# Taking 47 unread identity products off TensorE's queue in a two-block network on one core

## The reference, cut to what matters

```python
# first block, DEPTH = 2
for i in range(DEPTH):
    xn = rms_norm(h, norm_mix[i])
    h = h + (moba_attention(xn, ...) if i % 2 == 0 else rwkv7_time_mix(xn, ...))
    h = h + conv_ffn(rms_norm(h, norm_ffn[i]), ...)
x = rms_norm(h, norm_final)

# second block, DEPTH = 2
for l in range(DEPTH):
    h = rmsnorm(x, ln1_g[l]) * (1.0 + sc1) + sh1
    z = h @ w_in[l]
    xr, yr, q, k, v = jnp.split(z, splits, axis=-1)
    lru = rg_lru(causal_conv(xr, ...), ...) * jax.nn.gelu(yr)
    att = diff_attention(q, k, v, ...)
    x = x + g1 * (jnp.concatenate([lru, att], axis=-1) @ w_out[l])
    h = rmsnorm(x, ln2_g[l]) * (1.0 + sc2) + sh2
    f = swiglu(h, ...) if l % 2 == 0 else moe(h, moe_router[0], ...)   # 8 experts, top 2
    x = x + g2 * f
return rmsnorm(x, final_g)

def rms_norm(x, g):
    y = x * lax.rsqrt(jnp.mean(x * x, axis=-1, keepdims=True) + EPS)
    return y * g
```

## Time and profile before

| | before |
|---|---|
| median of 3 runs | 2081.14 us (2078.46 to 2083.44) |
| profiled execution, own time | 2088.03 us |
| its span | 2086.2 us |
| mean granted TensorE clock over the span | 0.985 |
| PE busy | 2030.1 us (97%), 12388 products in the trace |
| DVE, ACT busy | 1717.7 us (82%), 1257.7 us (60%) |
| HBM read | 531.47 MB, 255 GB/s over the span |

### The profile page before, as it was taken

One profiled execution on the slowest core, in us unless ns is written; L12 is line 12 of the kernel. 1 busy time (PEld: TensorE's weight loads), 2 busy tenths in 40 slices (PEclk: granted clock), 3 DMA queues, 4 the chain that ended last, 5 costly groups with the idle time before them and its releaser, 6 DMA issues. The chain is left out here.

```text
span 2086.2 us, 31412 instructions
## 1 busy us (share of the span) xinstructions
PE 2030.1 (97%) x12388; PEld 1759.5 (84%) x12389; DVE 1717.7 (82%) x1983; ACT 1257.7 (60%) x1282; POOL 45.5 (2%) x84
## 2 busy tenths in 40 slices
PE   9999999999899999999999999999999999999998
PEld 8889997988799988799998878888888788888876
DVE  6868887886788877778788788988898889989997
ACT  5564447643444356643445777777777777777775
POOL 0000000000000000000000000000000000000000
PEclk9999999998899999999999999999999999999999
DMA  7358862201477644378874259998999899999995
GB/s 279 122 209 278 308 228 76 103 22 44 179 282 263 246 136 169 124 293 302 305 258 147 101 210 374 360 368 324 377 354 370 321 367 361 355 350 366 362 343 212
DMA packets 79466, 534.53 MB, mean 256 GB/s; under 512 B 11840, under 2 KB 13120, under 8 KB 15584
## 3 DMA queue, kind: packets, MB, share of 16 engines
q1 hardware_dynamic: 71744, 481.04, 62.3%
q0 software_dynamic: 7440, 51.49, 6.7%
q10 hardware_dynamic: 144, 0.02, 0.0%
HBM read 531.47 MB, written 1.05 MB: 255 GB/s over the span
## 5 line engine op out<-in xcount | busy, mean ns | idle before, releaser
L2454 DVE TENSOR_TENSOR weights_lo<-ring,weights_hi 128x2048 fp32r<-128x2048 f32 x193 | 436.7, 2280 | 64.0 <-ACT weights_hi L2448 63.7
L826 PE MATMUL bank<-acts_hi,weights_hi 128*128 128x256 f32 x1584 | 454.2, 287 | 6.3 <-DVE acts_lo L425 3.8
L403 DVE TENSOR_TENSOR weights_lo<-ring,weights_hi 128x2048 fp32r<-128x2048 f32 x161 | 368.0, 2290 | 110.0 <-ACT weights_hi L393 108.8
L393 ACT CAST weights_hi<-ring 128x2048 fp32r<-128x2048 f32 x161 | 307.0, 1908 | 249.5 <-PE bank L826 224.6
L826 PE MATMUL bank<-acts_lo,weights_hi 128*128 128x256 f32 x1584 | 448.1, 283 | 0.0
L826 PE MATMUL bank<-acts_hi,weights_lo 128*128 128x256 f32 x1584 | 448.0, 283 | 0.0
L2448 ACT CAST weights_hi<-ring 128x2048 fp32r<-128x2048 f32 x192 | 367.3, 1917 | 80.8 <-PE bank L2969 50.1
L826 PEld LDWEIGHTS bank<-acts_hi,weights_hi 128*128 128x128 f32 x1584 | 303.6, 192 | 14.6 <-issue 11.5
L2969 PE MATMUL bank<-weights_hi,xg_hi 128*128 128x512 f32 x768 | 305.3, 398 | 7.1 <-issue 3.3
L826 PEld LDWEIGHTS bank<-acts_lo,weights_hi 128*128 128x128 f32 x1584 | 303.8, 192 | 2.6 <-issue 1.4
L826 PEld LDWEIGHTS bank<-acts_hi,weights_lo 128*128 128x128 f32 x1584 | 303.8, 192 | 0.0
(11 more groups left out here) (500 smaller groups left out, 2869.8 us busy)
## 6 DMA issues: line engine op xcount, KB each, us to landing
ring<-in_experts SPq DMA_DIRECT2D x192, 1024.0 KB, 6.6
ring<-in_dense SPq DMA_DIRECT2D x162, 1024.0 KB, 4.9
ring_more<-in_experts SPq DMA_DIRECT2D x96, 1024.0 KB, 6.7
ada<-in_ada POOLq DMA_DIRECT2D x48, 1024.0 KB, 5.2
silu_c<-in_c SPq DMA_DIRECT2D x3, 512.0 KB, 6.4
resid<-in_x SPq DMA_DIRECT2D x2, 512.0 KB, 4.3
out<-resid SPq DMA_DIRECT2D x4, 256.0 KB, 2.1
small<-in_consts SPq DMA_DIRECT2D x1, 649.5 KB, 10.3
```

What stands on the lines that cost most here:

```text
L393: nc.scalar.copy(split[0][:, n % SPLITS, :], ring[:, n % RING, :]).then_inc(hi_ready, 1)
L403: nc.vector.tensor_tensor(split[1][:, n % SPLITS, :], ring[:, n % RING, :], split[0][:, n % SPLITS, :].bitcast(F32), ALU.subtract).then_in ...
L826: ins = nc.tensor.matmul(bank[:, f * T:(f + 1) * T], split[w][:, m % SPLITS, k * 256 + f * P:k * 256 + (f + 1) * P], acts[x][:, k, :], sta ...
L2454: ins = nc.vector.tensor_tensor(split[1][:, at, lo:hi], place(j)[0][:, lo:hi], split[0][:, at, lo:hi].bitcast(F32), ALU.subtract)
```

## The change

All calls of `keep_busy`, the function itself and the arguments that carried its counts are taken out. No other line is changed.

```diff
@@ -431,15 +431,6 @@
-        def keep_busy(bank, count, wide=True):
-
-            for _ in range(count):
-                if wide:
-                    nc.tensor.matmul(pb[bank][:], ident, const("cos", 0, 2 * T), start=True, stop=True)
-                else:
-                    nc.tensor.matmul(pb[bank][:, 0:P], ident, ident, start=True, stop=True)
@@ -563,9 +554,8 @@
-            def pe(self, pe, before=0, behind=0):
+            def pe(self, pe):
                 done = self.normed
-                keep_busy(3, before)
                 for t in range(TT):
...
-                keep_busy(4, behind)
@@ -972,7 +961,6 @@
                     pe.wait_ge(early_in, 16)
-                    keep_busy(7, 10, wide=False)
                     norm.pe(pe)
@@ -1397,7 +1385,7 @@
                         pe.wait_ge(ada_read, tb + len(turns))
-                        norm.pe(pe, *((2, 3), (6, 2), (3, 2))[name])
+                        norm.pe(pe)
@@ -2119,7 +2107,6 @@
                     ins.then_inc(bonus_done, 1)
 
-                    keep_busy(7, 11)
                     pe.wait_ge(x_ready, 1)
                     pe.wait_ge(bonus_out, 2)
@@ -2617,7 +2604,6 @@
                         project(pe, n1 + 1, 1, 4, acts)
-                        keep_busy(3, 2)
                         if routes:
@@ -2630,7 +2616,7 @@
                             project(pe, n1 + c, c, 4, acts)
-                        norm.pe(pe, *((2, 2), (4, 1))[l])
+                        norm.pe(pe)
@@ -3021,7 +3007,6 @@
                 if kind in ("last", "extra"):
-                    keep_busy(4, 3, wide=False)
                     scatter_weighed(pe, n + 1)
@@ -3258,7 +3243,6 @@
                     sel = w3[2]
-                    keep_busy(7, 3)
                     pe.wait_ge(r_top, 1)
@@ -3266,9 +3250,7 @@
                     pe.wait_ge(normed, normed_made[0])
-                    keep_busy(7, 1)
                     gather(pe, 0, 2)
-                    keep_busy(7, 1)
                     all_passes(pe, pe_pass)
```

## The result

| | before | after |
|---|---|---|
| median of 20 runs each | 2082.13 us | 2088.80 us |
| ratio after/before, 95% interval | | 1.0032 [1.0023, 1.0041] |
| profiled execution, its span | 2088.03, 2086.2 us | 2084.07, 2082.3 us |
| mean granted clock in it | 0.985 | 0.978 |

The forecast was 2086.6 us with 5.5 us more than before; measured are 6.7 more. One of the 20 runs of after took 3315.45 us at a granted clock of 0.554 and is left out of the ratio; without it the median is 2088.32 us, 6.2 above that of before.

The account below looks back on a forecast made before the run. TensorE was taken to bound the kernel, 36 of the 42% of span the wait chain covers. Terms -3.4 + (1.7 + 1.9 + 2.3 + 0.6) + 0.8 + 0 + 1.6 + 0 = +5.5 on 2081.1 gave 2086.6 us; whole range 2078 to 2093.

Parts of the forecast that it names:

- mixers, both: Second block's mixers, at 862 and 1190: products stand on the path; transposes start 1.7 us earlier, twice: -3.4 us.
- norm 324: Norm at 324: cover lost, but a later wait for VectorE's mix swallows most: +0.6 us, from 0 to 1.7.
- norm 765: Norm at 765: 9.8 us with two norms in it, clock falls: +2.3 us, from 0 to 3.4.
- norm 880: Norm at 880: fall expected, dense products pay 1.5 us plus 0.2 for transposes: +1.7 us, between 0 and 3.3.
- norm 1095: Norm at 1095: stretch to the next product like that at 880, at 7.2 us: +1.9 us.
- the four norms: Norms at 324, 765, 880, 1095: products in spare time, removal wins nothing and loses clock cover: 6.5 us.
- start: Kernel's start: transposes and first products run at half speed, a later transfer wait swallows over 1 us: +0.8, 0 to 2.7.
- recurrent stage: Recurrent stage: about 1.1 us won at once, 32-wide products start at 1.2 GHz: 0, from -1.1 to +1.5 us.
- router: Router: without its three products the gather behind begins at 1.2 GHz: +1.6 us, from 0 to 3.4.
- First rival, the clock holds: At the norms transposes break the pauses, so their 6.5 us fall away: -1.0, or 2080 us; chance 20%.
- Second rival, no cover lost: Identity products cost path and cover nothing; mixers win 6.4 us, recurrent stage 1.1: 2073.6 us; chance 8%.
- Third rival, transposes do not hold the clock: Each norm is one bare pause of 7 to 10 us: +13.1, or 2094 us; chance 9%.

Follow-up runs that it names:

- mixers_moved: Kernel before with the mixers' four identity products moved, one behind each of the four norms' transposes: 2078.13 us, ratio 0.9981 [0.9972, 0.9989].
- lean: Kernel before less the unread products of the mixers, the first norm (324), the start and the end: 2080.27 us, ratio 0.9990 [0.9980, 0.9999].
- norms_out: Kernel before less only the identity products at the four norms: 2087.48 us, ratio 1.0027 [1.0016, 1.0038].
- rest_out: Kernel before less only the products at the start, in the recurrent stage, around the router and at the end: 2081.74 us, ratio 1.0004 [0.9995, 1.0013].
- mixers_out: Kernel before less only the identity products in the two mixers' output projections: 2085.76 us, ratio 1.0023 [1.0013, 1.0033].
- norms_kept: Kernel before less all unread products except those of the four norms: 2079.10 us, ratio 0.9989 [0.9980, 0.9998].
- norms_turned: Kernel before with each wide identity product at the four norms replaced by eight unread transposes: 2080.20 us, ratio 0.9994 [0.9983, 1.0005].
- recurrent_seven: Kernel before with 7 of the 11 products in the recurrent stage kept, all else unchanged: 2093.31 us, ratio 1.0052 [1.0033, 1.0070].

## Why the prediction was right

Its account was: the mixers' products cost path, the norms' cost nothing and hold the clock, and the second outweighs the first. By step, in us; the profile's column is one execution of after against one of before, each place measured against what precedes it; the last column is a kernel's difference in median, or, where it says so, a mean over the twelve profiles:

| place | predicted | profile of after | kernels |
|---|---|---|---|
| mixers, both | -3.4 | -1.7 and -1.7 | -3.5 (mixers_moved) |
| norm 324 | +0.6 | 0 | 0 (profiles of lean, norms_out) |
| norm 765 | +2.3 | +2.9 | |
| norm 880 | +1.7 | +2.7 | |
| norm 1095 | +1.9 | +1.0 | |
| the four norms | +6.5 | +6.6 | +7.2 (norms_out) |
| start | +0.8 | 0 | +0.7 (profiles) |
| recurrent stage | 0 | -0.3 | |
| router | +1.6 | +1.5 | +1.0 (profiles) |
| these three and the end | +2.4 | +1.2 | +1.4 (rest_out) |
| sum | +5.5 | +4.4 | +6.7 (the change) |

*Mixers.* Right to 0.1 us in the trace: the first product behind the transposes went from 867.34 to 863.62 and the transposes from 864.08 to 860.37, 3.7 us, of which 2.0 were there before the mixer. That the falls at 868 and 1196 may come or not was right too: after has the first alone; mixers_out has neither.

*Norms.* The mechanism is shown: falls where the products are gone (after, norms_out), none where they stay or transposes replace them (norms_kept, norms_turned). Three sizes were off. At 324 nothing is lost, where I had 0.6: the later pause swallows a fall whole. At 880 I had one fall, and there were two, the first over the transposes: the last product in front of the norm stood 3.7 earlier than before, the first feed-forward product only 2.27 earlier (884.74 against 887.01), which is 1.4 in the norm, and the second fall took 1.3 more. At 1095 the fall lay over the transposes only and ended in the pause behind them: the last product in front stood 1.03 earlier (1093.59 against 1094.62), the first behind 0.19 later, 1.2 lost, of which 0.25 is back ten microseconds on, and no dense product was at 1.2 GHz. I had charged each norm for dense products at half speed; the transposes at half speed were in my account with 0.2. They take 1.3 to 1.7 us more, and 0.7 (at 765) to 1.4 (at 880) of it reaches the next product. That the four come to 6.6, as forecast, is in part luck: 765 and 880 had been put too low by 0.6 and 1.0, 324 and 1095 too high by 0.6 and 0.9.

*First rival, the clock holds.* It fell at three norms. In the one that held in after (324), lean and norms_out show a fall, without a cost.

*Second rival, no cover lost.* Refuted by norms_out, 1.0027 [1.0016, 1.0038].

*Third rival, transposes do not hold the clock.* Refuted by norms_turned: no difference, where the rival would have it as slow as norms_out. The Trainium skill ("TensorE: Matmul & The Clock Gate", Part 4: PE-mode transpose), which says that transposes do not count as TensorE being busy in the way that brings the full clock, does not agree with the rows of norms_turned (1.00 over 872 to 889), if the transposes of this kernel, which the trace lists among the products, are what the page speaks of. The sign that I had named for this rival, 6 us or more at 0.50 behind a norm, was badly chosen: it did show in after, with 13.6 us at 765.

*Start.* In the pair of profiles nothing is lost. The transposes took 3.65 us where the earlier trace rows have 2.46, as foreseen, but TensorE's third block waits behind a transfer, and that came earlier in this execution; it ended ScalarE's wait at 22.86:

```profile
7.65 3.65 PE L565 MATMUL bank<-small,xn 128*128 128x128 f32 x16 [7.65 <-DVE xn L531]
...
22.86 1.90 ACT L393 CAST weights_hi<-ring 128x2048 fp32r<-128x2048 f32 x1 [3.75 <-DMA ring<-in_dense]
```

The pair misleads, though. The last product in front of the norm at 324 starts at 322.6 to 323.5 us in the seven profiles with the start's products (mean 322.87; before's is the latest) and at 323.0 to 324.2 in the five without (mean 323.53); from 47 us on the twelve take the same time to there. That is +0.7, near the 0.8, with a scatter as large.

*Recurrent stage.* TensorE stands 8.33 us where the 11 products were, and the 32-wide products begin 9.9 us behind the small transposes before, 8.6 after. Of these 1.2 won, the low clock (465.6 to 492.9, before 479.1 to 496.2) takes back 0.9 by the stage's first 64-wide products (482.83 to 480.78, where the transposes stood 1.71 earlier):

```profile
471.90 1.92 PE L2116 MATMUL bank<-xn,AD_first 32*32 32x32 f32 x64 [8.33 <-DVE xn L2273]
...
480.78 3.32 PE L2048 MATMUL bank<-AT,XT 64*64 64x64 f32 x29 [1.95 <-ACT AT L2168]
```

*Router.* The last product in front of it (L776, L765 in after) starts 3.40 us earlier than in before, the gather, at 1.2 GHz, 3.15 earlier, and the first expert's products 1.93 earlier (1224.02, before 1225.95): 1.5 lost, near the 1.6. Before is among the best here: five of the nine profiles with the router's products have a longer fall in front of the gather (6.8 us) and lose 1.1 by it. Mean against mean the products are worth +1.0.

```profile
1217.13 0.55 PE L2914 MATMUL bank<-Sel,acts_hi 128*128 128x256 f32 x1 [1.55 <-DVE Sel L3086]
...
1224.02 0.49 PE L2955 MATMUL bank<-weights_hi,xg_hi 128*128 128x512 f32 x1 [1.58 <-DVE xg_lo L3092]
```

*What stays open.* The places come to 4.4 us in the pair of profiles and to 4.6 with the means for start and router; measured are 6.2 to 6.7. By ratios the parts give +5.6 - 4.0 + 0.8 = +2.4 us, by medians +7.2 - 3.5 + 1.4 = +5.1; the whole is 6.7 [4.8, 8.5]. The whole less norms_kept would make the norms 9 us. Each interval is some 2 us to either side, so parts that add up and norms that cost more without the other products can't be told apart here. And nothing in the prediction saw the pause in the expert loop. That the whole change misses it is luck: with a list that put the loop where mixers_out and recurrent_seven have it, the forecast would have been short by some 8 to 11 us, going by these two.

## What to carry to other kernels

Ask of each unread product two things from the timeline: did anything that was ready wait behind it, and what is the idle piece in front of the next dense products once it is gone. Here those that something waited for cost 0.87 us each, those in front of dense products paid for themselves at three norms of four, and moving four from the first kind of place to the second was better than keeping or removing all. When a change in one place costs time in another that it does not touch, compare the loop's returns and the "issue" pauses before looking for a cause in the changed place.

## What the runs showed of the hardware that was not expected

- With four products fewer on TensorE's list in front of the expert loop, each of two returns of the loop has a pause of 3.2 to 3.8 us behind its sixth product, and the 48 triples from there take 50.1 to 52.3 us for 46.7. TensorE's waits of mixers_out from 1430 to 1440 (total, times, longest) name no engine, and one packet of 0.02 MB on the queue of instructions moved while TensorE stood (transfers from 1434.5 to 1437.0):

```profile
PE bank L2968 <- issue: 4.9, 2, 3.7
```

```profile
q8 instruction: 1, 0.02, 2.4%
```

  The Trainium skill ("Runtime: NRT & Kernel Launch", Instruction fetch mechanics) says that instructions come in blocks of 16 KiB, fetched ahead in order, and that a taken branch to a block that isn't there makes the engine wait for it. The packet and the pause fit that in part, since the pause stands six products behind the return and not at it. That the pause was a wait for this packet was not shown: such a packet moves some 3 us behind the first return in before (1443.05) and in mixers_moved (1434.94) too, where TensorE went on, and the number of them in a run doesn't tell the kernels with the pause (105 in both) from others (103 to 105).
- Falls of the clock at places that a change does not touch come in some profiles and not in others, at some 1.6 us each. From the first product of the third quarter at 867.34 to the end of the first mixer's projection it is 12.41 us in before, with the fall, and 10.83 in rest_out, which has the same list there and no fall. The two profiled executions lie 6 us above and 4.7 us below the medians of their kernels; the change is 6.7.
